# Summing 15 masked differences with four additions of halves in fp16, where one reduction in bf16 stood (a transformer block with product-key experts, one core)

## The reference

```python
s = jnp.einsum('thcd,hcnd->thcn', qb, sub_keys).astype(jnp.float32)
s_top, i_top = lax.top_k(s, PEER_TOPK)
cand = s_top[:, :, 0, :, None] + s_top[:, :, 1, None, :]
cand_idx = i_top[:, :, 0, :, None] * PEER_NKEYS + i_top[:, :, 1, None, :]
...
best, pos = lax.top_k(cand, PEER_TOPK)
eidx = jnp.take_along_axis(cand_idx, pos, axis=-1)
g = jax.nn.softmax(best, axis=-1)
...
h = jax.nn.gelu(jnp.einsum('td,thkd->thk', xb, ug).astype(jnp.float32), approximate=False)
return jnp.einsum('thk,thkd->td', (g * h).astype(x.dtype), vg)
```

## Time and profile before

| | |
|---|---|
| time, median of 3 runs | 1605.96 us (1601.4 to 1606.56) |
| profiled execution | 1601.73 us, its span 1599.9 us |
| mean granted clock of PE | 0.997 of full speed |
| busy share of PE, DVE, ACT, POOL | 99%, 80%, 39%, 33% |
| decoding of the first chunk on DVE | 539.80 to 559.89 us |
| last operation of the selection on DVE | 659.57 us |
| first low part made by DVE (tile 40) | 659.78 us |

### The profile page before, as it was taken

How to read it: one execution, slowest core, us unless ns; L and a number is a source line. 1 busy time by engine, 2 the same in 40 slices (tenths; PEclk the granted TensorE clock), 3 DMA queues, 4 the chain that set the end, 5 groups by cost and what they waited for, 6 DMA issues and landing times.

```text
span 1599.9 us, 24488 instructions
## 1 busy us (share of the span) xinstructions
PE 1578.9 (99%) x9566; PEld 1393.4 (87%) x9566; DVE 1276.5 (80%) x2390; ACT 630.1 (39%) x996; POOL 533.3 (33%) x261
## 2 busy tenths in 40 slices
PE   9999999999999999999999999999999999999998
PEld 7897977888989999989999998888878888888886
DVE  3024366345899999999998879999989999999997
ACT  5424345532222333445555333333334433434332
POOL 4433223351235789421010233333332232232200
PEclk9999999999999999999999999999999999999999
DMA  5332212135123669699998899999999999999972
GB/s 202 143 145 80 70 54 80 60 108 175 53 93 121 181 185 319 217 332 319 354 341 280 290 418 405 405 414 409 405 388 422 417 410 411 394 389 420 405 286 76
DMA packets 141633, 427.05 MB, mean 267 GB/s; under 512 B 11344, under 2 KB 73040, under 8 KB 120272
## 3 DMA queue, kind: packets, MB, share of 16 engines
q1 hardware_dynamic: 118224, 274.47, 47.5%
q0 software_dynamic: 23296, 151.04, 23.5%
HBM read 378.77 MB, written 46.14 MB: 266 GB/s over the span
## 4 chain that ended last, share of the span: by engine, by line
PE 62%; DVE 29%; DMA 4%; issue 3%; ACT 1%; POOL 0%; SPq 0%; DVEq 0%; ACTq 0%
PE bank L1437 19%; PE bank L1438 18%; PE bank L1439 18%; DVE acc L1311 4%; DVE uvb L1273 4%; DVE wlo L1265 3%; PE bank L1743 3%; DMA raw<-in_u 3%; DVE idx L1179 1%; DVE idx L1171 1%; DVE val L1170 1%; DVE val L1178 1%; DVE tmp L1172 1%; DVE cand L1214 1%; DMA raw<-in_uv 1%
## 5 line engine op out<-in xcount | busy, mean ns | idle before, releaser
L1437 PE MATMUL bank<-xhi,whi 128*128 128x352 f32 (+1 forms) x1408 | 488.5, 347 | 5.0 <-ACT hout L917 2.8
L1438 PE MATMUL bank<-xlo,whi 128*128 128x352 f32 (+1 forms) x1408 | 481.1, 342 | 0.0
L1439 PE MATMUL bank<-xhi,wlo 128*128 128x352 f32 (+1 forms) x1408 | 480.7, 341 | 0.0
L714 POOL DMA_INDIRECT uvb<-in_uv,eidx x128 | 212.1, 1657 | 551.5 <-DVE acc L1311 400.7
L896 ACT ACTIVATE whi<-raw 128x1024 fp32r<-128x1024 f32 x255 | 268.8, 1055 | 202.7 <-PE bank L1439 133.9
L1265 DVE TENSOR_TENSOR wlo<-raw,whi 128x1024 fp32r<-128x1024 f32 x215 | 262.6, 1222 | 52.9 <-ACT whi L896 52.6
L1437 PE MATMUL bank<-whi,ahi 128*128 128x512 f32 x762 | 300.1, 394 | 2.0 <-DVE wlo L1265 2.0
L1439 PE MATMUL bank<-whi,alo 128*128 128x512 f32 x762 | 297.4, 390 | 0.0
L1438 PE MATMUL bank<-wlo,ahi 128*128 128x512 f32 x762 | 297.2, 390 | 0.0
L1437 PEld LDWEIGHTS bank<-xhi,whi 128*128 128x128 f32 x1408 | 265.1, 188 | 22.2 <-DVE wlo L1265 4.4
L1439 PEld LDWEIGHTS bank<-xhi,wlo 128*128 128x128 f32 x1408 | 265.6, 189 | 15.4
(11 more groups left out here) (225 smaller groups left out, 1858.8 us busy)
## 6 DMA issues: line engine op xcount, KB each, us to landing
raw<-in_u SPq DMA_DIRECT2D x128, 512.0 KB, 6.5
raw<-in_uv SPq DMA_DIRECT2D x127, 512.0 KB, 9.7
g_scratch<-stage SPq DMA_DIRECT2D x48, 512.0 KB, 6.8
gl<-g_scratch SPq DMA_DIRECT2D x32, 768.0 KB, 8.7
raw<-in_w_in SPq DMA_DIRECT2D x22, 1024.0 KB, 4.8
h_scratch<-hout SPq DMA_DIRECT2D x96, 192.0 KB, 5.4
hl<-h_scratch SPq DMA_DIRECT2D x24, 768.0 KB, 11.5
raw<-in_w_q SPq DMA_DIRECT2D x6, 1024.0 KB, 4.8
```

Source lines behind the costliest of these rows:

```text
L714: nc.gpsimd.indirect_dma_start(out=uvb[:, r % UVB, :], out_offset=None, in_=a["uv"][:, :], in_offset=bass.IndirectOffsetOnAxis(ap=eidx[:, ...
L1437: mm(out, lh, rh, start=first, stop=False)
L1438: mm(out, lh, rl, start=False, stop=False)
L1439: return mm(out, ll, rh, start=False, stop=last)
```

## The change

`idf`, `didx`, `bposf`, `jf`, `ge`, `prod` and `cstb` are fp16 where they were bf16 (the same number of bytes, so no buffer moves). Each `tensor_reduce` over the 15 products is replaced by `sum_prod`: four additions of `prod` to itself. The first adds elements 8 to 14 of each row of 15 to elements 0 to 6 (128 rows of 7, 896 elements), the second 4 to 7 to 0 to 3 (512 elements), the third 2 and 3 to 0 and 1 (256), and the last writes the 128 sums to `sel` in fp32. There are 12 such sums, so 12 instructions go and 48 come, all on DVE and at the same places. Nothing else is changed on any engine.

```diff
-        idf = arena.buf("idf", [P, 16, TOPK], BF16)
-        didx = arena.buf("didx", [P, 16, TOPK - 1], BF16)
+        idf = arena.buf("idf", [P, 16, TOPK], F16)
+        didx = arena.buf("didx", [P, 16, TOPK - 1], F16)
...
-        ge = arena.buf("ge", [P, P, TOPK - 1], BF16)
-        prod = arena.buf("prod", [P, P, TOPK - 1], BF16)
+        ge = arena.buf("ge", [P, P, TOPK - 1], F16)
+        prod = arena.buf("prod", [P, P, TOPK - 1], F16)
...
+                def sum_prod():
+                    step(V.tensor_tensor(prod[:, :, 0:7], prod[:, :, 0:7], prod[:, :, 8:15], ALU.add))
+                    step(V.tensor_tensor(prod[:, :, 0:4], prod[:, :, 0:4], prod[:, :, 4:8], ALU.add))
+                    step(V.tensor_tensor(prod[:, :, 0:2], prod[:, :, 0:2], prod[:, :, 2:4], ALU.add))
+                    step(V.tensor_tensor(sel[:, :], prod[:, :, 0], prod[:, :, 1], ALU.add))
+
...
                     step(V.tensor_tensor(heads(prod), heads(ge), by_head(0), ALU.mult))
-                    step(V.tensor_reduce(sel[:, :], prod[:, :, :], AX, ALU.add))
+                    sum_prod()
...
                     step(V.tensor_tensor(prod[:, :, :], ge[:, :, :], row_of(1), ALU.mult))
-                    step(V.tensor_reduce(sel[:, :], prod[:, :, :], AX, ALU.add))
+                    sum_prod()
...
                     step(V.tensor_tensor(heads(prod), heads(ge), by_head(1), ALU.mult))
-                    step(V.tensor_reduce(sel[:, :], prod[:, :, :], AX, ALU.add))
+                    sum_prod()
```

More of the change, by code:

```diff
@@ L317, in program @@
         bpos = arena.buf("bpos", [P, PH, TOPK], U32)
-        bposf = arena.buf("bposf", [P, P], BF16)
-        jf = arena.buf("jf", [P, P], BF16)
-        ge = arena.buf("ge", [P, P, TOPK - 1], BF16)
-        prod = arena.buf("prod", [P, P, TOPK - 1], BF16)
+        bposf = arena.buf("bposf", [P, P], F16)
+        jf = arena.buf("jf", [P, P], F16)
+        ge = arena.buf("ge", [P, P, TOPK - 1], F16)
+        prod = arena.buf("prod", [P, P, TOPK - 1], F16)
         sel = arena.buf("sel", [P, P])
         hsum = arena.buf("hsum", [P, 2, TC, PH])
-        cstb = arena.buf("cstb", [P, 3, TOPK - 1], BF16)
+        cstb = arena.buf("cstb", [P, 3, TOPK - 1], F16)
         picks = arena.buf("picks", [P, 3, TC, P])
```

## The result

The changed kernel took 1634.28 us (median of 4 runs, 1632.5 to 1635.78), the kernel before 1605.13 (4 runs, 1601.4 to 1606.56). The ratio is 1.018, with a 95% interval of 1.0167 to 1.0193: 29 us slower. The profiled executions differ by 32.7 us in span (1632.6 and 1599.9), since the one of before lay at the low end of its runs.

The account below looks back on a forecast made before the run. PE, busy 99%, bounds the kernel and waits for DVE from tile 40 on. Waits of 53 us less 30, less 4.2 saved, made about 19; +18 on the 1606 median gave 1624 us, range 1612 to 1636.

Parts of the forecast that it names:

- Part 1: The additions by themselves on DVE: 1.83 us for a sum against 2.18 for the reduction, 4.2 us saved over twelve.
- Part 2, the waits: In the selection, additions and POOL's low parts exclude each other: 53 us of waits where there were 30.
- Part 2, the single chunks: Lag at each decoding's end: chunk 1 11.6 us, chunk 2 20.0, chunk 3 34; chunk 4 ends 18.8 late.
- the replay: DVE's and POOL's instruction lists of the selection played against each other by three rules: selection ends 18.8 us late.
- Part 3: Behind the selection: casts, POOL's low parts and the clock after the stall cost 0; the rest shifts with DVE.
- rival B: Additions in the selection held, and at one element per step: +24 to +30, 1626 to 1636 us; chance 0.08.
- Rival D: Additions in the selection not held, only part 1 counts, DVE 4.2 us early at tile 40: 1602 us; chance 0.15.
- Rival C: Additions in the selection held, but mostly in lucky places: +2 to +13, 1608 to 1619 us; chance 0.17.

Follow-up runs that it names:

- the layouts run: Changed kernel with a layout of its own in each of a chunk's three sums (rows of 16, second tile, dense rows): 1627.24 us.
- the rows of 16: Changed kernel with the product rows at a pitch of 16 elements in all twelve sums: 1625.1 us against 1602.89, ratio 1.0138.

## Why the prediction was right in direction and short in size

The forecast was 1624 us (1612 to 1636) and slower at 0.82; measured were 1634.3. Its place was right: PE waits once, ahead of tile 40, by what the selection is late. Step by step:

- **Part 1, "Twelve times 0.35 are 4.2 us saved": this step failed.** The durations were taken from products of 15 elements per row (1.23 us) and the one-hot tables, and fitted to two elements per step with any row pitch. With POOL idle they measure 0.95, 0.74, 0.63 and 0.39 for 0.69, 0.43, 0.29 and 0.29. The selection without POOL's reads puts the term at +8.5, not -4.2: 12.7 us of the 13.7 that were missed. The prediction named this case, "the pitch of 15 elements, which puts every other row at an odd place", with 2.63 us for a sum, close to the 2.71 + 0.13 measured, and set it aside because the products pass the same rows at two per step. But the products take in whole rows, and the additions a part of each row, a form for which no row stood; the layouts run shows that in this form the pitch counts.
- **Part 2, the waits: right.** It counted 53 us of waits where there were 30, so +23; measured are 54.4 for 30.4, +24. Operations that read two tensors are held, and casts, reductions never. With the zeros in place of POOL's subtraction no two-input operation is held, and with additions that cost no more than the reduction the loss is still 22 us.
- **Part 2, the single chunks: right only in the sum.** The first decoding ended 18.2 us late, not 11.6: the decoding took 38.6 us for 31.6, 3.4 more by the longer additions and 3.7 by two more holds (ten, 20.4 us, where the replay had eight). The prediction let a first addition of chunk 3 meet the six low parts; they were five, and they met the last operation of chunk 2, held for 12.53 us. That chunk so ended 43.7 us late (the cast behind it starts at 634.70, at 590.98 before) and not 20.0. Chunk 3 ended 45.0 late (665.67 for 620.64), and chunk 4, whose 12.44 us of waiting had been for this same run of low parts, won back 12.5. The replay also had no price for gathers: the addition at 594.60 was held for 3.4 us, through POOL's transfer of 593.43 and the low part behind it, not for 2.1. With the measured durations the replay was nearer: it gave 682, 675 to 681 and 662 to 668 in advance for kernels that measured 682.52, 679.23 and 664.47. But it missed the kernels in which POOL waits for itself, by 2 to 15 us, so I trust it for the sum of waits, not for places.
- **Part 3: right.** Nothing behind tile 40 wins anything back. The clock fell as expected, to 0.50 for 5 us, and the 2.2 us that it cost were taken from the waits for the transposes and tables.
- **The sum.** 18.8 was forecast, 32.5 measured in the profiled executions: 12.7 from part 1, 1 from part 2. The shift of 4.3 us from the profiled execution of before to its median, which I carried over, did not show in the changed kernel (1634.4 profiled, 1634.28 median), so the miss in the median is 10. That the time lies inside the stated range is in part luck: 32.7 us between the profiled executions is above its +30, and the carried 4.3 us put the top at 1636, just over the 1634.3 measured.
- **The rivals.** The time lies in the band of rival B (1626 to 1636), and its mechanism is half right: at a pitch of 15 the additions are slower than two elements per step, but not at one per step. The first takes less (0.95 us for its 1.09), the other three take more (0.74, 0.63 and 0.39 for 0.69, 0.43 and 0.29). Rival D, not held, is out: 8.5 us of own time alone would have been above it, and eleven of the 48 additions were held for about a whole low part or more, where fewer than two would have decided for it. Rival C, lucky places, did not come.

Two rules of the Trainium skill bear on this. The page "SBUF — State Buffer", section "Who interferes with whom", has a DVE instruction with two SBUF inputs contend with a GpSimd instruction that reads SBUF, not with one that only writes it. The runs agree, also where both inputs are halves of one tile (3.08 us for 0.95), and with the zeros, where no two-input operation waits. The "Vector Engine (DVE) Microarchitecture Reference", section 5.1, says of two 16-bit sources at two elements a cycle that 4-byte alignment makes no difference, and that a pair may span two rows of odd length. By that, with the 1.04 ns and 0.16 us of the prediction, 896 elements would take 448 steps, an estimate of 0.63 us, at either pitch. Measured are 0.93 us at a pitch of 15 and 0.70 at 16 (rows of 7 rounded up to four steps give 0.69), and for rows of 4 elements 0.75 and 0.43. The measurement decides.

**Open.** What lets a held operation of DVE in between two queued low parts of POOL is not settled. It was let in at every one in the kernel with the last chunk's additions; in five others one operation waited through four or five of them (9.83 to 12.53 us), and a cast through three in the layouts run (6.42 us at 629.38) and through two with the rows of 16 (4.62 us at 627.31). Nor was it tried why a pitch of 15 makes the additions longer, or why rows of 2 cost 0.39 us spaced at 16 and 0.29 dense.

## What to carry to other kernels

A reduction can be the cover under which another engine works (a cast, though it too reads one tensor, is not: it was held); before it is replaced by operations with two inputs, count the other engine's instructions that it hid, and price each at its full length. Here that price held however the waits were divided: breaking one wait of 12 us into single ones moved the end of the selection by 3 us at most. And take the duration of a halving tree from rows of its own form: a pitch of 15 elements made it longer than the reduction that it replaced (2.84 us with gaps for 2.18), a pitch of 16 not (2.04).

## What the runs showed of the hardware that I had not expected

- Additions in fp16 on parts of rows, 128 rows a partition, POOL idle: 7 elements of each row 0.93 us at a pitch of 15 and 0.70 at 16; 4 elements 0.75 and 0.43 (0.50 from a pitch of 15 to dense rows); 2 elements 0.63 and 0.39, 0.29 dense; one element to fp32 0.39 from spaced rows, 0.29 from dense ones.
- The same additions are a little longer where PE, the DMAs and POOL's zeros are at work beside them: 0.974, 0.779, 0.652 and 0.425 us on average, against 0.95, 0.74, 0.63 and 0.39 in PE's stall.
- DVE's operation can be held before POOL's low part begins: the one issued at 594.60 waited through 1.1 us of POOL's `DMA_DIRECT2D` and then the low part issued behind it. It is not always so: the addition at 605.42 took its bare 0.95 us beside a gather of POOL (604.94, 1.26 us), ahead of the low part of 606.22.
- A wait of POOL on its own last instruction costs POOL about 0.1 us (0.27 us of idle time ahead of the next gather, where there were 0.16) and lets DVE in between (in the kernel before with the bounds in PSUM, one wait of 11.85 us became single ones, the first three of 2.1 to 2.2), without a gain in the sum (33.8 us for 32.2).
